# The last three rounds of a weight ring: gate and up weights asked for behind the down weights, on a semaphore of their own

## The reference, cut to what matters

```python
expert_id = g_idx[..., None] * EXPERTS_PER_GROUP + top_i
combine = jnp.sum(jax.nn.one_hot(expert_id, N_EXPERTS) * top_w[..., None], axis=2)
for e in range(N_EXPERTS):
    he = jax.nn.silu(h2 @ w_gate[e]) * (h2 @ w_up[e])
    moe = moe + combine[..., e:e + 1] * (he @ w_down[e])
x = x + moe
y = rmsnorm(x, g_final)
```

## Time and profile before

| | |
|---|---|
| median of 3 runs | 432.7 us |
| the profiled execution | 431.91 us |
| its span in the trace | 430.1 us |
| PE busy | 411.3 us, 96% |
| DVE, ACT, POOL busy | 64%, 46%, 30% |
| SP's DMA queue (q1), share of 16 engines | 45.2% over the span |
| POOL's DMA queue (q0) | 12.4% over the span |

### The profile page before, as it was taken

One profiled execution on the slowest core, in us unless ns is written; L12 is line 12 of the kernel. 1 busy time (PEld: TensorE's weight loads), 2 busy tenths in 40 slices (PEclk: granted clock), 3 DMA queues, 4 the chain that ended last, 5 costly groups with the idle time before them and its releaser, 6 DMA issues.

```text
span 430.1 us, 7803 instructions
## 1 busy us (share of the span) xinstructions
PE 411.3 (96%) x2925; PEld 359.0 (83%) x2925; DVE 274.8 (64%) x663; ACT 197.8 (46%) x486; POOL 127.2 (30%) x210
## 2 busy tenths in 40 slices
PE   7899999999999999999999999999999999998992
PEld 3687999998876876787886899999989999998991
DVE  2856430905759898636457898655566777766984
ACT  5566230704565766332223634444544555554623
POOL 2012000200044324261001414333334555554443
PEclk9999999999999999999999999999999999999996
DMA  8851704506000039933224689999999989987321
GB/s 272 300 190 50 233 2 118 188 2 203 2 1 3 0 120 419 367 145 149 98 99 174 222 329 417 334 412 366 357 354 333 378 329 380 329 335 246 105 87 51
DMA packets 32074, 91.37 MB, mean 212 GB/s; under 512 B 11200, under 2 KB 11712, under 8 KB 27942
## 3 DMA queue, kind: packets, MB, share of 16 engines
q1 hardware_dynamic: 20790, 71.97, 45.2%
q0 software_dynamic: 11248, 18.93, 12.4%
HBM read 86.38 MB, written 26.01 MB: 261 GB/s over the span
## 4 chain that ended last, share of the span: by engine, by line
PE 74%; DMA 12%; DVE 6%; ACT 4%; issue 3%; POOL 0%; SPq 0%; DVEq 0%; ACTq 0%; POOLq 0%
PE ps L1224 18%; PE ps L834 10%; PE ps L836 9%; PE ps L835 9%; DMA region_w<-in_w_down 5%; DMA region_x<-h_rows,lists 5%; PE ps L1264 3%; PE ps L1265 2%; PE ps L1269 2%; PE ps L1217 2%; PE ps L998 2%; PE ps L963 2%; PE ps L1232 2%; DMA region_x<-in_x_prompt 1%; PE ps L981 1%
## 5 line engine op out<-in xcount | busy, mean ns | idle before, releaser
L1224 PEld LDWEIGHTS ps<-region_p,region_a 128*128 128x128 f32 x512 | 58.3, 192 | 1.0 <-DVE region_p L2105 0.4
L1224 PE MATMUL ps<-region_p,region_a 128*128 128x128 f32 x512 | 58.5, 275 | 0.0
L836 PE MATMUL ps<-region_a_r,region_w_r 128*128 128x288 f32 x192 | 56.5, 294 | 0.0
L834 PE MATMUL ps<-region_a_r,ring_r 128*128 128x288 f32 x128 | 40.5, 317 | 0.0
L835 PE MATMUL ps<-region_a_r,ring_r 128*128 128x288 f32 x128 | 37.7, 295 | 0.0
L836 PEld LDWEIGHTS ps<-region_a_r,region_w_r 128*128 128x128 f32 x192 | 36.0, 188 | 0.0
L1639 ACT ACTIVATE region_p<-ps,gffn_sb 128x128 f32<-128x128 f32 x116 | 31.6, 384 | 8.1 <-PE ps L1217 8.1
L1660 ACT ACTIVATE region_t<-ps 128x256 f32<-128x256 f32 x15 | 5.8, 384 | 53.2 <-PE ps L1224 53.2
L707 POOL DMA_INDIRECT region_x<-h_rows,lists x13 | 16.7, 1284 | 45.5 <-DVE slot_w L2208 33.5
L1224 PEld LDWEIGHTS ps<-region_p,ring 128*128 128x128 f32 x256 | 29.1, 192 | 0.8 <-DVE region_p L2127 0.5
L1224 PE MATMUL ps<-region_p,ring 128*128 128x128 f32 x256 | 29.3, 275 | 0.4 <-DVE region_p L2127 0.4
(11 more groups left out here) (381 smaller groups left out, 1030.9 us busy)
## 6 DMA issues: line engine op xcount, KB each, us to landing
region_a<-in_w_gate SPq DMA_DIRECT2D x8, 1024.0 KB, 9.5
region_a<-in_w_up SPq DMA_DIRECT2D x8, 1024.0 KB, 18.5
region_a<-in_w_down SPq DMA_DIRECT2D x8, 1024.0 KB, 18.9
region_w<-in_w_in SPq DMA_DIRECT2D x2, 2048.0 KB, 10.5
region_w<-in_w_out SPq DMA_DIRECT2D x2, 2048.0 KB, 7.9
ring<-in_w_gate SPq DMA_DIRECT2D x4, 1024.0 KB, 8.5
ring<-in_w_up SPq DMA_DIRECT2D x4, 1024.0 KB, 18.0
ring<-in_w_down SPq DMA_DIRECT2D x4, 1024.0 KB, 13.7
```

Source lines behind the costliest of these rows:

```text
L834: pe.matmul(out, lhs_hi, rhs_hi, start=first, stop=False)
L836: return pe.matmul(out, lhs_lo, rhs_hi, start=False, stop=last)
L1224: ins = pe.matmul(ps[:, 2 + b, (first + c) * P:(first + c + 1) * P], w[:, k, c * P:(c + 1) * P], xT[:, b, k, :], start=(k == 0), stop=(k = ...
```

## The change

1. `ring_loaded` is split: `gu_loaded[slot]` counts gate and up, `wd_loaded[slot]` counts down. PE waits for the first (32 per round), ACT's `wd_his` for the second (16 per round).
2. In the last three rounds of the loop (`i >= LATE`, 9 to 11) gate and up of e13, e14 and e15 are issued behind the down load of the same round, so behind its waits on `down_done` and on the rows of e(i+2).
3. To make room for four more semaphores, small ones elsewhere are merged (`hist_full` into `kc_full`, `hist_evac` into `ktok_evac`, `lam_dots` and `lam_made` into `lam_by_dve`, `early_onehot` and `oh_last_ready` into `onehot_late`), with the counts moved up.

```diff
+LATE = 9
...
-        ring_loaded = sems("ring_loaded", RING)
+        gu_loaded = sems("gu_loaded", RING)
+        wd_loaded = sems("wd_loaded", RING)
...
             def load_gate(slot, e, signal=None):
-                signal = signal or ring_loaded[slot]
+                signal = signal or gu_loaded[slot]
...
             def load_down(slot, e, signal=None):
-                signal = signal or ring_loaded[slot]
+                signal = signal or wd_loaded[slot]
...
             for i in range(E - RING):
                 sp.wait_ge(up_full, i + 1)
-                load_gate_up(i % RING, expert_at(i + RING))
+                if i < LATE:
+                    load_gate_up(i % RING, expert_at(i + RING))
                 if i >= 1:
                     sp.wait_ge(down_done, 2 * i)
                     sp.wait_ge(xg_loaded[i % 2], 16 * ((i + 2) // 2 + 1))
                     load_down((i - 1) % RING, expert_at(i - 1 + RING))
+                if i >= LATE:
+                    load_gate_up(i % RING, expert_at(i + RING))
...
-                pe.wait_ge(ring_loaded[u], it * 48 + 48)
+                pe.wait_ge(gu_loaded[u], it * 32 + 32)
...
-                act.wait_ge(ring_loaded[i % RING], 48 * (i // RING + 1))
+                act.wait_ge(wd_loaded[i % RING], 16 * (i // RING + 1))
...
-            pe.wait_ge(hist_evac, 1)
+            pe.wait_ge(ktok_evac, NT + 1)
...
-            pe.wait_ge(early_onehot, 1)
+            pe.wait_ge(onehot_late, 1)
...
-                pe.wait_ge(oh_last_ready, 1)
+                pe.wait_ge(onehot_late, 2)
```

More of the change, by code:

```diff
@@ L347, in build @@
         kc_evac = sem("kc_evac")
-        hist_full = sem("hist_full")
-        hist_evac = sem("hist_evac")
-        lam_dots = sem("lam_dots")
+        lam_by_dve = sem("lam_by_dve")
         lam_exp = sem("lam_exp")
-        lam_made = sem("lam_made")
         lam_spread = sem("lam_spread")
@@ L396, in build @@
         onehot_ready = sem("onehot_ready")
-        early_onehot = sem("early_onehot")
-        oh_last_ready = sem("oh_last_ready")
+        onehot_late = sem("onehot_late")
         first_half = sem("first_half")
@@ L642, in _ @@
                 pool.dma_start(kp_v[t] if t < PT else ks_v, k_st[0:rows(t), t, :]).then_inc(k_stored, 16)
-            pool.wait_ge(lam_made, 1)
+            pool.wait_ge(lam_by_dve, 2)
             pool.partition_broadcast(neglam[:, :], lam_t[0:1, 6:7]).then_inc(lam_spread, 1)
@@ L942, in _ @@
                                    ident[0:HIST, 0:HIST])
-            ins.then_inc(hist_full, 1)
+            ins.then_inc(kc_full, 1)
             for j in range(H + 1, 2 * H - 1):
@@ L1468, in _ @@
                 head_out(j)
-            act.wait_ge(lam_dots, 1)
+            act.wait_ge(lam_by_dve, 1)
             act.activation(lam_t[:, 2:4], lam_t[:, 0:2], ACT.Exp).then_inc(lam_exp, 1)
@@ L1825, in _ @@
             step(dve.tensor_tensor(lam_in[:, 0:2, :], lam_in[:, 0:2, :], lam_in[:, 2:4, :], ALU.mult))
-            dve.tensor_reduce(lam_t[:, 0:2], lam_in[:, 0:2, :], X, ALU.add).then_inc(lam_dots, 1)
+            dve.tensor_reduce(lam_t[:, 0:2], lam_in[:, 0:2, :], X, ALU.add).then_inc(lam_by_dve, 1)
             dve.wait_ge(consts_made, 2)
@@ L1847, in _ @@
                 dve.tensor_copy(k_st[0:n, t, :], ps[0:n, t % 4, :]).then_inc(ktok_evac, 1)
-            dve.wait_ge(hist_full, 1)
-            dve.tensor_copy(histT[:, :, :], ps[:, 3, 0:H * HIST].rearrange("p (g s) -> p g s", g=H)).then_inc(hist_evac, 1)
+            dve.wait_ge(kc_full, 3)
+            dve.tensor_copy(histT[:, :, :], ps[:, 3, 0:H * HIST].rearrange("p (g s) -> p g s", g=H)).then_inc(ktok_evac, 1)
             dve.wait_ge(lam_exp, 1)
             step(dve.tensor_tensor(lam_t[:, 4:5], lam_t[:, 3:4], lam_t[:, 2:3], ALU.subtract))
-            dve.tensor_scalar(lam_t[:, 6:7], lam_t[:, 4:5], -LAMBDA_INIT, None, ALU.add).then_inc(lam_made, 1)
+            dve.tensor_scalar(lam_t[:, 6:7], lam_t[:, 4:5], -LAMBDA_INIT, None, ALU.add).then_inc(lam_by_dve, 1)
             w_in_los(3)
@@ L2071, in _ @@
             dve.tensor_tensor(onehot_all[:, 0, 0:PT], iota_1[:, 0:PT], wide(rm[:, 0:PT, e0:e0 + 1].rearrange("p t a -> p (t a)"), [P, PT, P]),
-                              ALU.is_equal).then_inc(early_onehot, 1)
+                              ALU.is_equal).then_inc(onehot_late, 1)
             h2T_evac(NT - 1)
@@ L2108, in _ @@
             dve.tensor_scalar(oh_last[0:N_SAMPLE, :], iota_one[0:N_SAMPLE, :], rm[0:N_SAMPLE, PT, e0:e0 + 1], None,
-                              ALU.is_equal).then_inc(oh_last_ready, 1)
+                              ALU.is_equal).then_inc(onehot_late, 1)
             dve.tensor_tensor(onehot_all[:, 0, PT:NT], iota_1[:, PT:NT], wide(rm[:, PT:NT, e0:e0 + 1].rearrange("p t a -> p (t a)"), [P, 1, P]),
```

## The result

The changed kernel took 429.54 us (median of 8, 429.25 to 430.32) beside 432.53 us (8, 430.69 to 433.25) before: ratio 0.9946, 95% interval 0.9929 to 0.9964. That is 3.0 us faster where 1.0 was forecast (432.7 to 431.7), and it lies under the range.

The account below looks back on a forecast made before the run. PE was taken as the bound, its end hanging on expert 14's rows, with DMA nearly full. Profiled 431.91 + 0 + 0 + 0 - 1.0 = 430.9, plus 0.79 to the median: 431.7 us; range 430.5 to 433.0.

Parts of the forecast that it names:

- What bounds the kernel: Expert stretch: PE nearly always busy, only waits of 0.72 and 1.26 us to gain; end hangs on expert 14's rows.
- step 4: SP's queue runs empty about 0.8 us, so POOL's gather brings expert 14's rows sooner: 1.0 us gained.
- Step 1: Merged semaphores: same instructions, order and waits with other counts; cost 0, at most 0.2 us either way.
- Step 2: PE no longer waits for expert 7's down weights: 0.72 us go there, later waits take them back, 0 by itself.
- Step 3: Gate and up of experts 13 to 15 asked for 5.7 to 11.2 us later, still in time: cost 0.
- Case B: Both PE waits, ahead of expert 7 and at expert 14's rows, go wholly: 430.7 us; chance 0.18.
- Rule of the queues: DMA engines go round-robin between queues with work, so SP's order gives POOL 0 unless SP's queue runs empty.
- Rival A: SP's queue still holds work, for instance in the slowest engines; rows no sooner, 432.2 to 432.7 us; chance 0.28.
- Rival C: Burst of 4 MB from 381.8 on delays expert 14's rows up to 3.8 us: 434.6 to 436.5 us; chance 0.09.
- DVE's addition at 391.82: Next limit if both PE waits go: itself late for a gather, it would stop PE within some tenths.

Follow-up runs that it names:

- e15: Not a run: expert 15, the last expert; its gate and up weights (2 MB) are among the loads moved behind the down load.
- e0: Not a run: expert 0; times "after e0" count from the start of its gate and up, 242.98 us before, 242.96 after.
- e2: Kernel before with only SP's order changed (gate and up of experts 13 to 15 behind the down load), one semaphore per slot; ratio 0.9978.
- e8: Kernel before without the loads of expert 15's gate and up weights (2 MB); executed once, its time not compared.
- e1: Changed kernel with LATE = 12, so no gate/up load is moved; semaphore split and merges stay; ratio 1.000.
- e7: As a run: changed kernel, but late gate and up are asked for behind `down_done`, ahead of the wait for rows; ratio 0.9991. Elsewhere expert 7.
- e3: Changed kernel, but in the last three rounds gate and up come after the same waits and still ahead of the down load; ratio 0.9975.
- e9: Changed kernel with LATE = 10: gate and up of experts 14 and 15 deferred, expert 13's not; ratio 0.9982.
- e5: Changed kernel measured again, nothing altered; ratio to before 0.9961.
- f2: Changed kernel measured again beside two kernels with early sum rows, nothing altered; 429.95 us, ratio 0.9963; its profiled execution took 434.44 us.
- e12: As a run: changed kernel measured again beside three others on one chip, nothing altered; ratio to before 0.9978. In "e12's sum rows" expert 12.
- e14: As a run: changed kernel measured again, nothing altered; ratio 0.9955. In "e14's rows", gather, gate, up and down it is expert 14.
- f1: Changed kernel, but POOL asks for expert 12's sum rows right behind the gather of expert 14's rows; 430.29 us, ratio 0.997.
- e4: Changed kernel with LATE = 11: only expert 15's gate and up are moved behind the down load; ratio 0.9963.
- e6: Changed kernel with LATE = 1: gate and up behind the down load in all rounds from i = 1 on; ratio 0.9977.
- e10: Changed kernel (LATE = 9), but expert 15's gate and up are the last loads, behind expert 15's down; 429.41 us, ratio 0.9953.
- e13: As a run: LATE = 9 with expert 15's gate and up behind its down, measured again; 430.97 us, ratio 0.995. Elsewhere expert 13.
- f3: Changed kernel with expert 12's sum rows asked for early and expert 15's gate and up behind its down; 429.41 us, ratio 0.9957.
- e11: Changed kernel with LATE = 11 and expert 15's gate and up behind its down, experts 13 and 14 as before; ratio 0.9966.

## Why the prediction was wrong

The two limits, put side by side over all traces. The gather of e14's rows was asked for at 129.2 after e0 in all of them but before (130.2), e2 (129.9) and e8 (130.9):

| run | e15's gate asked for, us after e0 | e14's rows land | e12's sum rows land | e15 starts | e15 to end |
|---|---|---|---|---|---|
| e1 | 127.1 | 150.9 | 156.1 | 168.06 | 18.64 |
| before | 128.1 | 151.3 | 156.9 | 168.48 | 18.64 |
| e7 | 131.0 | 150.7 | 156.9 | 167.90 | 18.65 |
| e3 | 133.7 | 147.6 | 156.0 | 165.93 | 19.71 |
| e9 | 134.4 | 148.1 | 156.5 | 165.90 | 20.27 |
| e2 | 136.8 | 145.3 | 156.7 | 166.66 | 19.56 |
| changed | 136.8 | 143.1 | 154.3 | 165.96 | 18.58 |
| changed (e5) | 136.9 | 144.3 | 154.4 | 165.91 | 18.58 |
| changed (f2) | 137.2 | 150.7 | 157.7 | 167.86 | 19.57 |
| changed (e12) | 137.5 | 145.3 | 156.6 | 165.93 | 20.25 |
| changed (e14) | 137.7 | 145.0 | 156.3 | 165.90 | 20.08 |
| f1 | 137.8 | 142.3 | 145.3 | 165.91 | 18.63 |
| e4 | 138.3 | 142.6 | 153.1 | 165.97 | 18.58 |
| e6 | 139.8 | 143.8 | 154.1 | 167.49 | 18.59 |
| e10 | 142.4 | 144.9 | 150.5 | 165.96 | 18.61 |
| e13 | 142.3 | 145.5 | 156.7 | 165.93 | 20.39 |
| f3 | 142.3 | 143.0 | 145.8 | 165.92 | 18.59 |
| e11 | 142.7 | 142.8 | 148.8 | 166.34 | 18.63 |
| e8 | never | 144.1 | 150.7 | 168.45 | 18.57 |

**What bounds the kernel: right**, as far as it went. The end hung on e14's rows, and the two waits named were those that went. The DMA rows were read too simply, see step 4.

**Step 1, merged semaphores, 0: right.** Up to e6, ahead of the first wait that the split removes, the starts after e0 in e1 and in the changed kernel are those of before within 0.05 us, e0 itself starts at 242.96 instead of 242.98 in the changed kernel, and e1's ratio is 1.000.

**Step 2, the split by itself 0: nearly right.** Its local size was too small. The wait reads 0.72 us, but 0.95 us went with it (0.90 in the start, 0.08 in the shorter first pass, less the 0.02 us by which all of this trace is early). e1 keeps 0.4 of it in the trace, since asking sooner did move e14's rows by 0.4 us, and nothing that the timing can tell.

**Step 3, late but in time: right.** No run shows a wait of PE for gate or up weights. e15's up weights landed at 394.1 (151.1 after e0), in e10 at 158.6, and PE wants them at 166. The 22.5 us taken as the longest landing was never reached by a moved load; the three up loads took 15.2, 14.5 and 13.9 in the changed kernel. One sentence of the step is wrong: that no down load is later than before. e15's stands behind e15's gate and up now and lands 2.1 us later, which no engine waited for.

**Step 4, what it gives the rows, 1.0 us: this step failed.** The rows came 8.2 us sooner. The step's term hung on a gap of 0.8 us in SP's queue, and two of its readings were wrong. The first is that "the loads served ahead of e14's rows are the same 6 MB or fewer", so that only an empty SP queue could help. After the change e14's down and e15's gate and up landed behind the rows, as shown above. The second is that SP's queue is full up to the last landing of its loads. A gap like the 0.8 us that the step worked out is there, about half a microsecond long, in 381:381.5 of the changed kernel:

```profile
q0 software_dynamic: 48, 0.10, 50.4%
q1 hardware_dynamic: 1, 0.00, 0.1%
```

But in the 4.5 us ahead of it (376.5:381), while e14's up weights were still under way up to 381.7, SP's queue kept the engines less than half busy:

```profile
q1 hardware_dynamic: 97, 0.62, 46.1%
```

The trace of before had the sign of this too. In 368.6:384 us, where by the landings SP's queue was full throughout, the share of busy DMA engines in 40 slices (tenths, 9 is 90% or more) was

```profile
DMA  5569754999988999999999999999987654454998
```

with stretches of mostly four to seven tenths at both ends. The first ends at 371.3, just behind the issue of e15's gate at 371.04. SP's queue in 370.3:371.3 and in 371.3:372.3:

```profile
q1 hardware_dynamic: 26, 0.15, 36.1%
```
```profile
q1 hardware_dynamic: 59, 0.31, 82.8%
```

So that load was moving at once, with e14's up weights, asked for at 360.44, on their way until 379.2. The likely reading is that some of the 16 engines had nothing left to do while the slowest still worked off their part; the trace gives only the mean over the 16, so this is not shown engine by engine.

What is shown is what the gather pays for e15's 2 MB. Without them its rows land 7.2 us sooner (e8). With them it hangs on when they are asked for. From 2 us ahead of the gather to 1.8 us behind it, the gather takes 21 to 22 us (before, e1, e7). At 4.5 and 5.2 us behind it 18.4 and 18.9 (e3, e9), and from 6.9 us on 13.1 to 16.3, in twelve of thirteen traces. The thirteenth is f2, with 21.5 us at a distance of 8.0. The 8 us are well more than the 2.5 that PE had to gain, so the bound of the gain was PE's waits, case B, and not the gap.

**Case B, 1.98 us if both waits go: the right case with a chance of 0.18, and its size too small.** The traces give 2.6 us: 0.95 at e7, 0.08 at e13, whose rows had come with 0.06 us to spare, 1.48 at e14, where the wait reads 1.26, and 0.06 behind e15's start. The range ended at 430.5, so that B with these costs, 432.7 - 2.6 = 430.1, was outside it. The remaining 0.6 us down to 429.54 are within the spread of the medians (before 431.4 to 432.5 in six series); in the four later series the changed kernel's median was 429.8 to 430.95.

**Rule of the queues.** e14's gather took 21.1 us before, and 13.2 in e8 without e15's 2 MB. The rule that I cited from the Trainium skill (DMA: Bandwidth & Descriptors, "Queues, rings and completion order"), engines going round between queues that have work, does not contradict that. I used it as if there were one ring per queue; the same section has a ring per queue and engine, and with that it does not give the 0 that I drew from it, since one engine can be done with SP's loads while another is not. No run here shows a single ring.

**Rival A, the rows do not come sooner:** its mechanism, SP's queue still at work in the slowest engines, is nearer to what the rows show than step 4, but its result, rows that come no sooner, shows in only one trace of the changed order, f2. **Rival C, slower: wrong.** No kernel timed here is shown to be slower than before, and no trace has e14's rows later after e0 than before. Whether the burst had a part in f2 is open.

**What I had not seen: the second limit.** I named DVE's addition at 391.82 as the next in line, but the one that counts is that behind e12's sum rows. The table gives its rule for this kernel: where they land 11.0 us or more ahead of e15's start (11.0 in e7, more in eleven others), the stretch behind e15 is 18.6 us; where it is 10.2 us or less (f2, e2, e3, e14, e9, e12, e13), it grows to 19.6 to 20.4 us, the more the later they land, and PE waits 0.7 to 1.6 us for DVE. Before, PE reached e15 2.5 us later and did not meet it. In f1 and f3 the gather is asked for 6 to 7 us sooner and the wait is gone, which bears out the link in one trace each. What stays open is why the gather of these rows takes 13 us in one execution and 19.6 in another of the same kernel (e10, e13), and why e14's rows do so in f2. Which of the 16 engines is late, and at what, the trace does not tell.

## What to carry to other kernels

Where the DMA engines are near full, ask of each prefetch what it is served beside: a load that is needed 40 us later cost the gather that was needed next 7 us. It still cost 2 to 8 us when asked for 2 to 5 us behind that gather; from 7 us behind it, in the last round, no such cost showed in twelve of thirteen traces. Do not take a queue's last landing for the time that the queue is busy; look at the share of busy engines in slices. Once a wait goes, look for the next one with all engines moved up: here it took back up to 1.8 of 2.5 us in some executions. And compare one trace with one trace only where several of each agree: the same kernel had the same gather at 13.9 and at 21.5 us.

## What the runs showed of the hardware beyond that

- A wait of TensorE costs more than its idle time reads: 0.72 us read and 0.95 us gained, 1.26 read and 1.48 gained. The first matmuls behind the gap take longer (64 in 7.38 us instead of 7.30, eight transposes in 1.09 instead of 1.04). And the overlap with the work ahead is lost: without a wait the transposes start 0.15 us before the modelled end of the pass ahead (391.84 against 384.69 + 7.30). For e14 that is 1.26 + 0.05 + 0.15 = 1.46.
- The spread of the medians comes in part from the kernel's start. In four traces (e1, e14, f1, f2) PE waited 1.1 to 1.4 us for ACT at 10 us; the granted clock was then 0.86 of 2.4 GHz in the mean of 12 to 24 us, that is part of it at 1.2 GHz, and e0 started at 244.8 to 245.2 us. In the other traces that wait was 0 to 1.2 us, the clock 1.00, and e0 started at 242.2 to 243.9. In e3 the wait was 1.2 us too and the clock stayed at 1.00, so the wait alone does not decide it. The rows of f1 and of f3 for that stretch (start:end, length, busy time of PE, PEld, DVE, ACT and POOL, clock, DMA share, GB/s):

```profile
12.00:24.00 12.00, 10.89 (x47) 8.72 (x48) 8.51 (x19) 4.42 (x9) 0.00 (x0) 0.86 0.80 262
```
```profile
12.00:24.00 12.00, 11.39 (x57) 9.42 (x58) 9.66 (x20) 5.25 (x10) 0.00 (x0) 1.00 0.87 296
```

These 2 to 3 us are as large as the whole effect of the change, and fall on either kernel. Part of the first measured gain of 3.0 us may be such chance. Of the executions whose mean granted clock was 0.993 or more, the medians in the four later series were 431.2 to 431.6 us for before and 429.5 to 430.1 us for the changed kernel, in each series 1.4 to 1.9 us less; in the first series they were 429.5 us for the changed kernel, and of before no clocks are on record there. This division was made after the fact, and a wait of PE lowers the mean clock too, so it is a hint and no measurement.
